# In the gathers of a one-core kernel, VectorE and ScalarE do their share of each background unit two rows after TensorE's

## The reference, cut to what matters

```python
v1, i1 = lax.top_k(s1, PEER_TOPK)
v2, i2 = lax.top_k(s2, PEER_TOPK)
...
u = jnp.take(expert_u, ic, axis=0)
act = jax.nn.gelu(jnp.einsum('cd,ced->ce', xc, u).astype(jnp.float32), approximate=False)
vv = jnp.take(expert_v, ic, axis=0)
return jnp.einsum('ce,ced->cd', (gc * act).astype(vv.dtype), vv)
```

## Time and profile before

| | |
|---|---|
| median of three runs | 5476.44 us |
| profiled execution | 5502.99 us, its span 5501.2 us |
| PE busy | 3615.6 us, 66% |
| VectorE busy | 2942.9 us, 53% |
| ScalarE busy | 816.3 us, 15% |
| GpSimd busy | 1960.8 us, 36% |
| granted TensorE clock, mean | 0.731 |
| DMA | 1321.25 MB, 240 GB/s over the span |
| costliest group | L1293 matmuls, 3501.1 us in 9164 |
| indirect DMAs | 2048, 1073.87 MB |

### The profile page before, as it was taken

One profiled execution on the slowest core, in us unless ns is written; L12 is line 12 of the kernel. 1 busy time (PEld: TensorE's weight loads), 2 busy tenths in 40 slices (PEclk: granted clock), 3 DMA queues, 4 the chain that ended last, 5 costly groups with the idle time before them and its releaser, 6 DMA issues.

```text
span 5501.2 us, 34464 instructions
## 1 busy us (share of the span) xinstructions
PE 3615.6 (66%) x9742; PEld 1773.4 (32%) x9742; DVE 2942.9 (53%) x5957; ACT 816.3 (15%) x1938; POOL 1960.8 (36%) x2058
## 2 busy tenths in 40 slices
PE   5778646887567667757575467751478885554566
PEld 1256413554212234315321111120256653221111
DVE  1211696547945766652476874540342223778766
ACT  1110112211101211111111110110131101111111
POOL 0000355435534656640254464430100000544665
PEclk8879757888688788865766567776688877666556
DMA  4235689988889999980487699870200003877999
GB/s 178 72 89 151 234 275 337 336 300 315 298 324 359 373 359 379 386 317 31 176 321 270 227 374 346 334 271 21 75 1 1 1 0 127 331 283 274 361 370 329
DMA packets 481787, 1321.25 MB, mean 240 GB/s; under 512 B 39884, under 2 KB 138444, under 8 KB 481088
## 3 DMA queue, kind: packets, MB, share of 16 engines
q0 software_dynamic: 294912, 1073.87, 52.4%
q1 hardware_dynamic: 179672, 219.30, 12.2%
q10 hardware_dynamic: 7016, 25.88, 1.3%
HBM read 1314.08 MB, written 1.17 MB: 239 GB/s over the span
## 4 chain that ended last, share of the span: by engine, by line
issue 22%; PE 20%; DMA 11%; POOL 8%; DVE 6%; SPq 2%; ACT 2%; another core or an unknown queue 1%; DVEq 0%; ACTq 0%; POOLq 0%
PE ps L1293 19%; POOL arena L2324 8%; DMA arena<-in_peer_up,arena 4%; DVE arena L637 2%; DMA arena<-in_peer_v,arena 2%; DVE arena L650 1%; DMA arena<-in_ada_w 1%; DMA arena<-in_peer_u,arena 1%; ACT arena L1878 1%; DVE ps L650 1%; SPq L2444 1%; DMA arena<-in_w_mod 1%; DMA arena<-mod_scratch 1%; PE ps L1299 1%
## 5 line engine op out<-in xcount | busy, mean ns | idle before, releaser
L1293 PE MATMUL ps<-arena 128*128 128x512 f32 (+12 forms) x9164 | 3501.1, 537 | 1555.9 <-DMA arena<-in_peer_up,arena 525.2
L1293 PEld LDWEIGHTS ps<-arena 128*128 128x128 f32 (+5 forms) x9164 | 1677.8, 216 | 3323.9 <-issue 2356.4
L650 DVE SCALAR_TENSOR_TENSOR arena<-arena,ps 128x1024 f32<-128x1024 f32 x1024 | 1245.2, 1216 | 394.2 <-DMA arena<-in_peer_down,arena 179.2
L2324 POOL DMA_INDIRECT arena<-in_peer_down,arena x768 | 723.4, 942 | 1715.1 <-DVE arena L654 965.9
L2324 POOL DMA_INDIRECT arena<-in_peer_up,arena x768 | 730.2, 951 | 476.7 <-issue 216.0
L650 DVE SCALAR_TENSOR_TENSOR ps<-arena,ps 128x512 f32<-128x512 f32 x1016 | 764.5, 753 | 190.9 <-DMA arena<-in_peer_up,arena 89.6
L1878 ACT ACTIVATE arena<-arena 128x128 f32<-128x128 f32 (+4 forms) x1251 | 448.3, 385 | 2586.2 <-issue 786.5
L2324 POOL DMA_INDIRECT arena<-in_peer_u,arena x256 | 240.5, 939 | 945.0 <-DVE arena L654 842.4
L637 DVE TENSOR_TENSOR arena<-ps,arena 128x512 f32<-128x512 f32 (+2 forms) x182 | 125.5, 690 | 636.5 <-PE ps L1293 598.9
L637 DVE TENSOR_TENSOR arena<-arena 128x16 f32<-128x16 f32 (+9 forms) x399 | 266.9, 669 | 222.4 <-DMA arena<-arena 148.1
L1878 ACT ACTIVATE arena<-ps 128x256 f32<-128x256 f32 (+3 forms) x341 | 172.9, 507 | 1274.8 <-PE ps L1293 896.8
(11 more groups left out here) (35 smaller groups left out, 563.4 us busy)
## 6 DMA issues: line engine op xcount, KB each, us to landing
arena<-in_w_mod SPq DMA_DIRECT2D x24, 2048.0 KB, 9.4
arena<-in_w_in SPq DMA_DIRECT2D x72, 512.0 KB, 5.5
arena<-in_w_pq SPq DMA_DIRECT2D x12, 2048.0 KB
arena<-in_ada_w SPq DMA_DIRECT2D x12, 2048.0 KB
arena<-in_w_in SPq DMA_DIRECT2D x8, 2048.0 KB, 20.0
arena<-in_w_out SPq DMA_DIRECT2D x8, 2048.0 KB, 7.7
arena<-mod_scratch ACTq DMA_DIRECT2D x30, 512.0 KB, 8.5
arena<-in_peer_down,arena POOLq DMA_INDIRECT x768
```

What stands on the lines that cost most here:

```text
L650: self.e.scalar_tensor_tensor(o, a, s, b, op0, op1, accum_out=accum).then_inc(*(inc or self.inc(self.S.vec)))
L1293: return self.e.matmul(o, l, r, start=start, stop=stop)
L2324: self.e.indirect_dma_start(out=o, out_offset=None, in_=table, in_offset=bass.IndirectOffsetOnAxis(ap=idx.bitcast(U32), axis=0)).then_inc( ...
```

## The change

A walk of no engine (`Walk(None, K)`) goes through the program first and writes down, for each weave, how many units follow each row and at which rows units are needed. All engines then follow these counts. VectorE and ScalarE have `late = 1`, and the three gathers pass `delay=DELAY`, 2: they put the units of a row on a list and do them once two further rows stand behind it, except at needed rows (every 32nd) and at the last, where the list is emptied. PE, GpSimd and SyncE, and the weaves that aren't gathers, have no delay.

```diff
+DELAY = 2
...
+    late = 0
...
-    def weave(self, front, back, rate, rings=("front", "back"), slots=(None, None), done=()):
+    def weave(self, front, back, rate, rings=("front", "back"), slots=(None, None), done=(), delay=0):
+        if self.e is None:
+            return self.plan(front, back, rate, done)
         ring, slot = self.ring, self.slot
+        counts, needed = self.K.plans[self.woven]
+        self.woven += 1
+        pending = []
+        for s, n in enumerate(counts):
             self.ring = self.rings[rings[0]]
             self.slot = self.slots[slots[0]] if slots[0] else slot
+            next(front, "end")
+            pending.append(n)
+            wait = 0 if s in needed or s == len(counts) - 1 else self.late * delay
+            while len(pending) > wait:
+                self.ring = self.rings[rings[1]]
+                self.slot = self.slots[slots[1]] if slots[1] else slot
+                for _ in range(pending.pop(0)):
+                    next(back, "end")
+                    self.units += 1
+        self.ring, self.slot = ring, slot
+
+    def plan(self, front, back, rate, done):
+        done, owed, hold, steps, left = set(done), 0.0, 0, 0, True
+        counts, needed = [], set()
+        while True:
             need = next(front, "end")
             if need == "end":
                 break
             steps += 1
+            counts.append(0)
+            if need:
+                needed.add(steps - 1)
             owed = min(owed + (rate(steps) if callable(rate) else rate), 8.0)
             while left and ((need and need not in done) or (owed >= 1.0 and steps >= hold)):
-                said = unit()
+                said = next(back, "end")
                 owed -= 1.0
-                self.units += 1
+                counts[-1] += 1
...
+        self.K.plans.append((counts, needed))
...
-                   ctx_then_x(queries), RATE0, done=done)
+                   ctx_then_x(queries), RATE0, done=done, delay=DELAY)
...
 class Vector(Walk):
+    late = 1
...
 class Scalar(Walk):
+    late = 1
...
+        K.plans = []
+        Walk(None, K).main()
```

More of the change, by code:

```diff
@@ L144, in __init__ @@
         self.rows, self.units = 0, 0
-        self.base = 0
+        self.base, self.woven = 0, 0
     def wait_ge(self, sem, value):
@@ L240, in weave @@
                         done.update(said[1:])
-            assert not need or need in done or not left, need
+            assert not need or need in done, need
+        counts.append(0)
         while left:
-            left = unit() != "end"
-            self.units += 1
-        self.ring, self.slot = ring, slot
+            left = next(back, "end") != "end"
+            counts[-1] += 1
+        self.K.plans.append((counts, needed))
     def run(self, stage):
@@ L538, in queries_then_mod @@
             yield from self.modvec(2, pm.free[0][0], range(12))
-        self.weave(self.gather([0, 1], tables, gelu, [(1, 0, 5), (1, 0, 5)]), queries_then_mod(queries), RATE1, done=done)
+        self.weave(self.gather([0, 1], tables, gelu, [(1, 0, 5), (1, 0, 5)]), queries_then_mod(queries), RATE1, done=done, delay=DELAY)
         self.folded(6)
@@ L587, in main @@
         self.weave(self.gather([0, 1], (A["peer_u_2"], A["peer_v_2"]), gelu2, [(2, 0, 5), (2, 0, 5)]),
-                   last_queries(queries), RATE2, done=done)
+                   last_queries(queries), RATE2, done=done, delay=DELAY)
         self.store()
```

## The result

The changed kernel took 5551.28 us in the median of four runs (5529.34 to 5563.64), the kernel before 5478.73 us (5467.74 to 5490.61): 1.2% slower, ratio 1.012 with an interval of 1.0095 to 1.0145. The forecast was 5447 us, within 5400 to 5512. The sign was wrong, and the time lies above the range, 15 us above the end of its first rival.

A forecast was written before the change was run, and what follows sets the result against it. No engine was taken to bound the whole span; VectorE, PE or DMA bound single stretches, and only gathers could change. Gains of 58 us against costs of 29 gave -29 us from 5476.4: 5447 us, range 5400 to 5512.

The forecast's parts named there:

- first rival: `attend` and `x_mix`: supply runs dry, POOL waits for PE; costs 74 us, gains 14 to 45, +29 to +60; chance 0.20.
- The sum: Whole kernel: costs of 29 us less gains of 58 us, -29 us from 5476.4, giving 5447 us.
- (e): `modulate` and `qkv` of `x_mix`: 13 steps where PE waits for later VectorE steps; cost 20 us (0 to 39).
- What bounds the kernel: First gather: VectorE bounds top-16 rows, PE and DMA `gates`, DMA `modvec`; no engine is busy for the whole span.
- The plan at nothing: All weaves: the common plan gives the counts each engine found for itself, so it costs nothing.
- (a): Scores, L916, first gather: VectorE's waits for PE shrink as two fronts fit in; gain 24 us (14 to 32.7).
- (b): Copies, L654, first gather: two fronts could cover VectorE's 13 waits for PE; gain 19 us (0 to 38).
- (c): `gates` at the slow rate and VectorE's wait for ScalarE's tile copy: mostly hidden by DMA; gain 10 us (0 to 41).
- (d): `gates` at the fast rate and `project`: only VectorE's two-row lead after `project` counts; gain 5 us (0 to 14).
- (f): `attend`, sixteen heads: three rows bound by release to landing, supply not short; cost 5 us (0 to 26).
- SyncE's loads at nothing: `modvec`: loads hang on VectorE marks two rows later, but VectorE waits for PE there anyway; no cost.
- (g): Gathers two and three: work from the two rows before now stands in six bursts; cost 4 us (0 to 9).

The follow-up runs named there:

- e11: Changed kernel, DELAY = 2 only in rows 0 to 64 and 169 to 235 of the first gather; 5480.83 against 5492.35 us before, ratio 0.9981.
- e1: Changed kernel with DELAY = 0, the common plan alone; 5358.49 against 5357.26 us for the kernel before, ratio 1.000.
- e4: Changed kernel, DELAY = 2 only in first-gather rows 65 to 68, 124 to 130, 165 to 168, 281 to 341; ratio 1.0088 to the kernel before.
- e8: Changed kernel, DELAY = 2 only in rows 69 to 123 of the first gather (`attend`); 5367.86 against 5364.23 us before, ratio 1.0003.
- e3: Changed kernel, DELAY = 2 but none in first-gather rows 65 to 68, 124 to 130, 165 to 168, 281 to 341; ratio 1.0039 to the kernel before.
- e10: Changed kernel, DELAY = 2, five `us` buffers instead of four, three row buffers instead of four; 5499.78 us, ratio 1.0011 to the kernel before.
- e2: Changed kernel with DELAY = 1 instead of 2; ratio 1.0015 to the kernel before.
- e9: Changed kernel, DELAY = 0, five `us` buffers instead of four, three row buffers instead of four; 5490.88 us, ratio 1.0007 to the kernel before.
- e7: Changed kernel, DELAY = 0, three `us` buffers instead of four, four `ds`; 5591.3 us, ratio 1.0431 to the kernel before.

## Why the prediction was wrong, point by point

**The step that failed.** The price of PE's lag behind VectorE. The sum had it at 20 us for `x_mix` (e) and at nothing for the other VectorE-led rows; the runs showed 33 to 35 us and 17 to 21 us. Against it the sum set gains of 58 us, of which e11 shows 10.

**What bounds the kernel.** Held. VectorE bounds the top-16 rows, PE and DMA `gates`, DMA `modvec`, and the changed kernel keeps these stages: 152 for 157 us in `gates`, 223 for 221 us in rows 236 to 280.

**The plan at nothing.** Held (e1).

**(a) Scores, 24 us.** The mechanism held and the size was off. The wait before L916 was to fall from 43 to under 15; after has

```profile
DVE arena L939 <- PE ps L1316: 17.6, 5, 4.5
```

But a wait that goes isn't time won one for one: of 26 us less waiting, rows 0 to 65 became 8 us shorter and rows 198 to 211 6 us, and e11 gives 10 us for the whole term (2 to 19), where its low end was 14.

**(b) Copies, 19 us.** Wrong. They were to fall under 20 us:

```profile
DVE arena L677 <- PE ps L1316: 32.4, 10, 10.3
```

In ten waits, where there were thirteen, VectorE lost nearly as much (38.0 in the earlier trace rows) and the longest is 10.3 us instead of 7.4. I had noted that PE had itself waited for VectorE just before; in that case PE starts the copies' matmuls two rows later too, and VectorE gains nothing. No run tries that reason by itself; what the trace shows is 6 us less waiting, for a term of 19.

**(c) `gates` at the slow rate and the tile's copy, 10 us.** Wrong, but small: 1944 to 2373 us takes the same 429 us as in the earlier trace rows, and the wait for ScalarE's copy is 21.1 us, 17.4 before. Rows 128, 256 and 384 are needed rows, but the copy stands before the list is emptied; what is left in front of it on ScalarE was not looked at.

**(d) `gates` and `project`, 5 us.** `gates` became 5 us shorter by VectorE's marks and `project` 10, but the next rows took 24 back: VectorE was only ahead, nothing was won. Between level rows, 129 to 193, the stretch is 9 us longer (12 in e4 against e1), and 65 to 97, with the `qkv` of the context, 6 us longer (7). This is what I left out: the VectorE-led rows 65 to 68, 124 to 130 and 165 to 167 were in no term; (e) counted those of `x_mix` only. The price was 17 us for rows 65 to 193 (`attend` and `gates` in it), and 21 in e4, which delays only the VectorE-led rows.

**(e) VectorE-led steps of `x_mix`, 20 us.** The mechanism was right and the price too low: between level rows 35 us in the profiled executions and 33 in e4 against e1, for the 13 steps 2.7 and 2.5 us each and not 1.5. One input was too small: I took a landing of 5.0 to 6.1 us from pieces of the chain in rows where little runs beside the gather. e1, whose trace has the landings, shows for `in_peer_up` in rows 280 to 341

```profile
DMA to landing us min/median/max: 4.8/6.4/15.1
```

With 6.4 my own sum misses 1.8 us a step, 23 us in all (an estimate), so that is a small part. The rest I put down to what the sum left out: I had set the landing against three rows of VectorE, from PE's release, and in the norm above POOL had been idle for 6.30 us by then. A row needs 2.5 us of POOL's 2.8, so it can hardly catch up afterwards. That the lost issues make the difference is argued; what is shown is VectorE's waits for landing, 12 us before and 78 after. Ask how long POOL's issues stop, not only whether the next landing comes late.

**(f) `attend`, 5 us.** 2 us in the profiles, and 0.03% in e8 (at most 13 us): held.

**SyncE's loads at nothing.** Near enough: PE's wait for the loads of `modvec` (`in_w_mod`) rose from 66 to 98 us over the program, but e3, which keeps the delay in those rows, is within 5 us of e1 in rows 225 to 289.

**(g) Bursts, 4 us.** None to be seen: by the same rows the second gather takes 6 us less and the third 7 us less than before.

**The sum.** Gains were 58 us and would have been some 10 (e11). Costs were 29 us and are some 76: 1.2% is 66 us, and the gain of 10 on top of it. By e4, 0.88% or 47 us of them is in the rows where VectorE leads, and its profile has them in rows 257 to 353 (33) and 65 to 193 (21). e10 puts nearly all down to the `us` supply. My first rival had place, sign and mechanism, at 0.20; its costs of 74 us lie near the 76 partly by luck: (e) at its high end, 39, was near what was measured, but (f) and (g), 35 us, are hardly to be seen in the times and stand where the other VectorE-led rows should. Its price of 29 to 60 us fell short of 66 because it set gains of 14 to 45 us against them. I preferred the gains because VectorE's waits for PE are large in the profile, and I discounted them by "half" without asking of each which engine had been late first.

Two numbers of the working are wrong and change little: the forecast's range lies 24 us below 5449, not 18, so its share of "same" is a little larger than 0.10; and 2327 to 2411 us holds 31 rows by VectorE's products, so the floor is 2.7 us a row and some 420 us of the first gather are above it, not 380.

**What stays open.** e3 leaves 0.39% with the delay off where VectorE leads. Its profile has all of it, 19 us more than e1, in rows 65 to 129, where `attend` is; where the delay is switched off (162 to 165 and 280 to 284) it takes 13 and 11 us longer, but between the level rows around them (129 to 193, 257 to 289) only 3 and 2 us of that are left. Yet the times of e8 allow `attend` alone at most 13 us. e10 shows that with a fifth buffer nothing of it is left that can be told, so it too seems to hang on the supply, in rows that I can't name for certain.

## What to carry to other kernels

An order of work that lets one engine run behind another takes its depth from the buffers that the two hand on to a third. Before engines are set apart by n steps, count for each buffer how many steps its supply may lag, and find the stages in which the engine that now runs ahead waits for the one set back: there the lag works against it. Price that by how long the issuing engine stops, if it is nearly full otherwise.

Of a wait, ask which engine was late first. Only a wait for work that the other engine could have begun earlier by itself can be won by the shift; set it there alone, as e11 does.

A wait of POOL "for PE" rose by some 256 us with a cost of 0.15% (e2 against e1) and fell by half with no gain (e9): in a queue that issues in order, a standstill is booked before whichever instruction stands at its head, under the name of the engine that this one waits for. The sum of these rows says more than one of them, but it misleads too: in e7, 4.3% slower, the rows for PE and for L673 on `arena` add up to 489 us, less than the 604 of e1, and a third row (VectorE's share of `us`, 274.6 us) holds the rest. The length of the stretch measures a loss, if it is cut where both kernels have done the same work.

## What the runs showed of the hardware

The same kernel before took 5357 to 5364 us beside e1 to e8 (chips 1 and 2) and 5479 to 5498 us in the other runs (chips 1 and 13 where the record names them), 2.1 to 2.6% more. Chip 1 stands in both groups, so the record does not show that the chip makes the difference; what does is open. The gather shows where it lies: in rows 480 to 511, with little beside it, e1 has

```profile
2295.00:2374.00 79.00, 55.35 (x62) 14.16 (x62) 61.61 (x96) 12.30 (x33) 56.18 (x60) 0.63 1.02 406
```

406 GB/s and 2.5 us a row, where the earlier trace rows has 371 GB/s and, by the same count of 31 rows, 2.7 us, both with DMA all but full. The instructions of the gather are nearly as long in both: VectorE's product 1216 ns before and 1217 in e1, POOL's fetch 939 and 937 ns (median, `in_peer_up`), PE's 128x512 matmul 829 and 811 ns at mean granted clocks of 0.731 and 0.743. A difference of one profile of each kernel is therefore only to be used within one group of runs, and even there with care: e1 and e3, on one chip and in one series, have `attend` in 147 and 164 us.

The Trainium skill's page DMA: Bandwidth & Descriptors, in its section on where the 436 GB/s come from, puts the HBM side at about 358 GB/s for a core, as half of a stack's 716 GB/s. The 406 GB/s above, kept over 79 us by a kernel that runs on one core, are more than that, so this half is no bound here.
